# Seven products of half size in the gates of the merge, halved transforms and banded pooling

## The chip, the cores and the metric

The kernel runs on one core of a Trainium2 chip. The metric is the device time of one execution in microseconds; of the kernel before there are three runs, and their median counts. One more execution was profiled; all rows below come from it.

## The reference

Two blocks of two layers each are computed in float32 on 256 context and 256 latent tokens of width 1024. The change touches the second block only, whose mixer takes, in each of its two layers, the normed and modulated tokens `h` and a wide input projection and joins three branches under gates:

```python
k, v, q, u, f, gt = jnp.split(h @ w_in[l], IN_SPLITS, axis=-1)

def multiscale_pool(u, pool_w, pool_scale):     # windows of 2, 4, 8, 16 tokens
    ...
    pooled = (win_sum / cnt - ug).astype(u.dtype)
    y = jnp.einsum('btgc,gcd->btgd', pooled, pool_w).reshape(B, T, POOL_WIDTH)
    return y * pool_scale

def fourier_mix(f):
    ...
    y = jnp.fft.fft2(fg, axes=(1, 3), norm='ortho').real

def merge_branches(o_attn, pool_in, four_in, gate_in, ...):
    g_a, g_p, g_f = jnp.split(jax.nn.sigmoid(gate_in), N_BRANCHES, axis=-1)
    y = (g_a * (o_attn @ w_br_attn)
         + g_p * (multiscale_pool(pool_in, pool_w, pool_scale) @ w_br_pool)
         + g_f * (fourier_mix(four_in) @ w_br_four))
    return y @ w_out
```

The gates are the last 3 x 1024 columns of `h @ w_in`. After the mixer comes a feed-forward part (`w_up`, a convolution over tokens, `w_down`). In layer 0 all 512 tokens pass through mixer and feed-forward, in layer 1 only the 256 latent ones.

## The kernel before

Values lie transposed: features on the 128 partitions, tokens in columns. `hT` holds the normed tokens (8 tiles of 128 features), `brT` the branches (tiles 0 to 3 attention, 4 and 5 pooling, 6 and 7 Fourier), `yT` the merged result. `ps` is PSUM with 8 banks of 512 words. Weights come through a ring of slots of 1 MB in `ring_mem`, loaded by the SP queue; a strip is loaded when the last user of its slot has counted up `strips_used`. Order between engines is written by hand with semaphores. Each engine runs its own program: `merge_tensor` on PE (TensorE), `merge_scalar` on ACT (ScalarE), `merge_vector` on DVE (VectorE), and so on, layer after layer.

In a layer the input projection comes first, then attention in units (lines 1189 to 1337), and with its last unit the other branches:
- `spectra_tensor` (line 1337), issued between the transposes and the values of the last attention unit: for each of two channel tiles and each sequence (two in layer 0, one in layer 1) two matmuls of 512 columns, cosine and sine transform over 256 tokens each.
- `branches_tensor`: pooling as matmuls with a 256 x 256 table (line 1350, `poolm`, two halves of the partitions side by side); `second`, the transform over channels (lines 1360, 1361), for one sequence at a time; the pool weights (line 1366). VectorE copies spectra and pooled values (lines 2363, 2369), ScalarE the results into `brT` (lines 1920, 1925).
- The merge: four turns t of two column tiles m. For each, three gates j of eight matmuls with all tokens (line 1383: 512 columns in layer 0, 256 in layer 1) into banks 0 to 2, and the three branches, 4 + 2 + 2 matmuls (line 1395), into banks 3 to 5. ScalarE makes the sigmoid (line 1936) into `gts`, VectorE multiplies (line 2382) and adds (lines 2385, 2386) into `yT`.
- `out_tensor` (line 1421) with `w_out`, for half of the tokens at a time.

The up stage behind it (`up_tensor`, line 1454) already uses a seven-product form of Strassen's scheme (Winograd's variant). A strip of 1024 x 256 weights is split into four blocks a11, a12 (first 128 columns) and a21, a22, the tokens into two halves. Each of 22 steps does seven products P1 to P7 of four matmuls at half of the tokens, from sums of weight blocks (two by VectorE, lines 2468 and 2469; two by GpSimd, lines 2676 and 2677) and sums of token tiles made once. ScalarE copies P1 (line 1951), and VectorE gathers the results in six sums (lines 2434 to 2442), then does a convolution (line 2451) and the gating. Its products alternate between two sets of four banks, so step f+1 writes one set while f's is gathered.

The values of the last attention unit are line 1311, its copies lines 1906 and 2353. `hT` is completed by ScalarE at line 512.

Of the kernel before, what the change touches and what calls it, by code (L numbers as in the profile page):

```python
# [148 lines left out]
def build(nc, w, const, out):  # L149
# [5 lines left out]
    with ctx:  # L155
# [104 lines left out]
        q_raw = yT[:, 0:4, :]  # L260
        kb = at(T)
        k_rot = at(LAT)
        vb = at(NG * 128).rearrange("p (g c) -> p g c", g=NG)
        ub = at(NG * 256).rearrange("p (g c) -> p g c", g=NG)
        fb = at(NG * 256).rearrange("p (g c) -> p g c", g=NG)
        sc = at(4 * T).rearrange("p (u h t) -> p u h t", u=2, h=2)
# [4 lines left out]
        b_tables = at.at  # L271
        if mla_end > b_tables:
            raise ValueError("the tables lie over the pairs")
# [4 lines left out]
        dftm = at(2 * 512).rearrange("p (s t) -> p s t", s=2)  # L278
# [4 lines left out]
        gts = at(3 * T).rearrange("p (b t) -> p b t", b=3)  # L283
        brg = at(3 * T).rearrange("p (b t) -> p b t", b=3)
# [49 lines left out]
        br_full, br_act_kept, br_dve_kept = sem("br_full"), sem("br_act_kept"), sem("br_dve_kept")  # L334
# [211 lines left out]

        HG_FIRST, HG_ORDER = (2, 3, 0, 4, 1), (2, 4, 0, 3, 1)

        @block.sync
        def _(sp):  # L550
# [80 lines left out]
            for l in range(2):  # L631
# [11 lines left out]
                def merge(j, t):  # L643
                    if j < 3:
                        return [(strip(f"merge{l}", j, 8), wk["w_in_2"][l][:, :, bass.ds(t * 256 + (1280 + j * 1024), 256)])]
# [514 lines left out]
        def base(l):  # L1160
            return dict(unit=16 + 12 * l, ptf=32 + 24 * l, kt=16 + 12 * l, pv=8 + 12 * l, rot=5 + 3 * l, qj=1 + 3 * l, pvk=8 + 4 * l,
                        full=5 * l, act=5 * l, dve=3 + 5 * l, br=12 * l, brd=6 * l, bract=4 * l)
# [168 lines left out]

        def spectra_tensor(pe, l):
            n = 0
            for ct in range(2):
                for s in range(l, 2):
                    for st in range(2):
                        mm = PE.matmul(ps[:, 2 + n, :], fb[:, 2 * s + st, ct * 128:ct * 128 + 128], dftm[:, st, :],
                                       start=st == 0, stop=st == 1)
                    mm.then_inc(br_full, 1)
                    n += 1  # L1340

        def branches_tensor(pe, l):

            b = base(l)
            seqs = range(l, 2)
            for gp in range(2):
                for s in seqs:
                    for st in range(2):
                        for e in range(2):
                            mm = PE.matmul(ps[e * 64:e * 64 + 64, (1, 6)[gp], s * 256:s * 256 + 256],  # L1350
                                           ub[:, 2 * s + st, (2 * gp + e) * 64:(2 * gp + e) * 64 + 64], poolm[:, st, 2 * gp + e, :],
                                           start=st == 0, stop=st == 1)
# [15 lines left out]

        def merge_tensor(pe, l):
            b = base(l)  # L1370
            n, c0 = T - CTX * l, CTX * l
            name = f"merge{l}"
            pe.wait_ge(pv_kept, raised(b["pvk"] + 4))
            with pe.Fori(0, 4) as t:
                for m in range(2):
                    for j in range(3):
                        if m == 0:
                            ring.wait_loaded(pe, name, j, t)
                        if j == 0:
                            pe.wait_ge(gates_ready, raised(t * 6 + (3 * m + 24 * l)))  # L1380
                        wj = strip(name, j, 8)
                        for k in range(8):
                            mm = PE.matmul(ps[:, j, 0:n], wj[:, k, m * 128:m * 128 + 128], hT[:, k, c0:T], start=k == 0, stop=k == 7)  # L1383
                        if m == 0:
                            mm.then_inc(mg_full, 1)
                        else:
                            strip_used(mm)
                    if m == 0:
                        ring.wait_loaded(pe, name, 3, t)
                        pe.wait_ge(br_act_kept, b["bract"] + 4)  # L1390
                    pe.wait_ge(mg_read, raised(t * 2 + (m + 8 * l)))
                    wj = strip(name, 3, 8)
                    for j, (k0, k1) in enumerate(((0, 4), (4, 6), (6, 8))):
                        for k in range(k0, k1):
                            mm = PE.matmul(ps[:, 3 + j, 0:n], wj[:, k, m * 128:m * 128 + 128], brT[:, k, c0:T],  # L1395
                                           start=k == k0, stop=k == k1 - 1)
                        if j < 2 or m == 0:
                            mm.then_inc(mg_full, 1)
                strip_used(mm)

        def wait_merge(eng, l, t, m, bank):
# [1371 lines left out]
```

## Time and profile before

| | us |
|---|---|
| median of three runs | 2563.21 (2562.05 to 2564.33) |
| profiled execution | 2560.08 |
| span of its trace | 2558.3 |
| PE busy | 2489.7 (97%) |
| DVE busy | 1195.6 (47%) |
| ACT busy | 604.2 (24%) |
| POOL busy | 269.0 (11%) |

PE is TensorE's matmuls and PEld its weight loads, which run beside them. A float32 matmul shows as two PE records and two PEld records, and their times overlap those of the next: what a matmul costs in a stream is read from the starts of groups or from the length of a stretch, not from the mean duration of a record. "Idle before" names what ended an idle time. The merges are at 1389.9 to 1609.6 us (layer 0) and 2182.0 to 2292.5 us (layer 1), the up stages at 1666.5 to 1939.9 and 2323 to 2466 us.

### The profile page before, as it was taken

Reading aid. Unit: us, or ns where it says so; the run is one execution under the profiler, and the core shown is the slowest. Engines: PE = TensorE matmul, PEld = TensorE weight load, DVE = VectorE, ACT = ScalarE, POOL = GpSimd, SP = SyncE. Lnnn points to the kernel's source line nnn. Section 1 sums busy time; section 2 is a strip of 40 time slices with the busy share of each in tenths; the row PEclk is TensorE's granted clock in tenths of the full one; section 3 lists DMA queues with packets and bytes.
Section 4 is the critical chain, followed back from the end, with each engine's and each line's share of the span. In section 5 each row is a group of like instructions: output and inputs, shape, how many; then the busy total and the mean of one; then the engine's idle time right before and its main releaser. Section 6 shows DMA issues by size and latency. Waiting matters only on the chain.

```text
span 2558.3 us, 32946 instructions
## 1 busy us (share of the span) xinstructions
PE 2489.7 (97%) x13364; PEld 1947.6 (76%) x13364; DVE 1195.6 (47%) x2007; ACT 604.2 (24%) x1205; POOL 269.0 (11%) x194
## 2 busy tenths in 40 slices
PE   7999999999999898999999999999999999999999
PEld 3688888888887577867885444788885687889998
DVE  3176696696786613343234111256663014116961
ACT  3123233232332113143224000121211023113211
POOL 0011211122121000000000000112120000003410
PEclk9999999999999999999999999999999999999999
DMA  9443343443334042410520222233243132354662
GB/s 357 165 171 139 118 148 116 142 169 115 131 110 137 26 131 82 132 50 23 142 66 1 66 66 90 82 90 85 83 111 85 51 83 66 113 175 124 173 178 63
DMA packets 320673, 284.88 MB, mean 111 GB/s; under 512 B 27137, under 2 KB 300169, under 8 KB 320057
## 3 DMA queue, kind: packets, MB, share of 16 engines
q1 hardware_dynamic: 318810, 279.08, 35.4%
q0 software_dynamic: 1280, 4.20, 0.5%
q8 instruction: 75, 1.23, 0.2%
q14 instruction: 29, 0.24, 0.0%
q10 hardware_dynamic: 479, 0.13, 0.0%
HBM read 280.24 MB, written 3.15 MB: 111 GB/s over the span
## 4 chain that ended last, share of the span: by engine, by line
PE 79%; DVE 13%; issue 3%; ACT 2%; DMA 1%; SPq 0%; DVEq 0%; ACTq 0%
PE ps L1454 11%; PE ps L1383 10%; PE ps L733 7%; PE ps L1533 5%; PE ps L793 4%; PE ps L1521 4%; PE ps L1421 3%; PE ps L1395 3%; PE ps L784 2%; PE ps L917 2%; PE ps L935 2%; PE ps L1012 2%; PE ps L831 2%; DVE arena L2451 2%; DVE arena L2090 2%
## 5 line engine op out<-in xcount | busy, mean ns | idle before, releaser
L1383 PE MATMUL ps<-hT,ring_mem 128*128 128x512 f32 (+1 forms) x768 | 250.3, 486 | 0.0
L1383 PEld LDWEIGHTS ps<-hT,ring_mem 128*128 128x128 f32 x768 | 145.9, 190 | 101.3 <-issue 91.4
L2382 DVE TENSOR_TENSOR arena<-ps,arena 128x512 f32<-128x512 f32 (+1 forms) x48 | 26.8, 558 | 291.3 <-PE ps L1395 291.3
L733 PE MATMUL ps<-xT,ring_mem 128*128 128x256 f32 x672 | 159.8, 381 | 1.6 <-DVE ring_mem L2134 1.4
L733 PE MATMUL ps<-hT,ring_mem 128*128 128x256 f32 x672 | 158.8, 379 | 0.0
L733 PEld LDWEIGHTS ps<-xT,ring_mem 128*128 128x128 f32 x672 | 126.7, 190 | 22.8 <-issue 3.8
L733 PEld LDWEIGHTS ps<-hT,ring_mem 128*128 128x128 f32 x672 | 126.1, 190 | 18.9 <-issue 2.9
L1454 PE MATMUL ps<-hT,arena 128*128 128x256 f32 (+1 forms) x704 | 131.6, 331 | 6.9 <-ACT hT L512 6.9
L831 PE MATMUL ps<-arena,K_c 128*128 128x128 f32 x896 | 120.5, 289 | 11.8 <-ACT K_c L1717 11.7
L831 PEld LDWEIGHTS ps<-arena,K_c 128*128 128x128 f32 x896 | 116.9, 195 | 18.9 <-ACT K_c L1717 11.5
L1454 PE MATMUL ps<-arena 128*128 128x256 f32 (+1 forms) x704 | 129.6, 327 | 0.0
L2391 DVE SCALAR_TENSOR_TENSOR xT<-ps,mod_b,xT 128x256 f32<-128x256 f32 (+1 forms) x60 | 23.6, 427 | 216.0 <-PE ps L1521 88.0
L1454 PEld LDWEIGHTS ps<-hT,arena 128*128 128x128 f32 x704 | 110.7, 193 | 17.5 <-issue 7.5
L1454 PE MATMUL ps<-hT,ring_mem 128*128 128x256 f32 (+1 forms) x704 | 123.0, 327 | 0.0
L443 DVE RECIPROCAL rstd<-root 128x256 f32<-128x256 f32 (+2 forms) x17 | 28.2, 1659 | 199.6 <-ACT root L416 198.5
L2673 POOL TENSOR_TENSOR arena<-ring_mem 128x512 f32<-128x512 f32 x4 | 5.2, 1296 | 1101.5 <-DMA ring_mem<-in_w_up_dram 1101.5
L1521 PE MATMUL ps<-arena,ring_mem 128*128 128x512 f32 (+1 forms) x352 | 115.8, 491 | 2.2 <-DVE arena L2461 2.2
L1454 PEld LDWEIGHTS ps<-arena 128*128 128x128 f32 x704 | 109.7, 191 | 9.1
L1533 PE MATMUL ps<-arena,ring_mem 128*128 128x256 f32 (+1 forms) x704 | 116.6, 327 | 0.0
L1454 PEld LDWEIGHTS ps<-hT,ring_mem 128*128 128x128 f32 x704 | 107.9, 191 | 9.7 <-issue 0.6
L1533 PEld LDWEIGHTS ps<-arena,ring_mem 128*128 128x128 f32 x704 | 106.5, 191 | 10.1 <-issue 1.1
L793 PE MATMUL ps<-ring_mem,hT 128*128 128x256 f32 x512 | 113.0, 379 | 0.0
(316 smaller groups left out, 4302.5 us busy)
## 6 DMA issues: line engine op xcount, KB each, us to landing
ring_mem<-in_w_mod_dram SPq DMA_DIRECT2D x24, 2048.0 KB, 7.7
ring_mem<-in_w_up_dram SPq DMA_DIRECT2D x88, 512.0 KB, 5.2
ring_mem<-in_hg_w_in_dram SPq DMA_DIRECT2D x40, 1024.0 KB, 5.2
ring_mem<-in_w_in_dram SPq DMA_DIRECT2D x30, 1024.0 KB, 5.4
ring_mem<-in_w_down_dram SPq DMA_DIRECT2D x16, 1408.0 KB, 7.0
ring_mem<-in_ada_w_dram SPq DMA_DIRECT2D x8, 2048.0 KB, 7.7
ring_mem<-in_mla_w_in_dram SPq DMA_DIRECT2D x9, 1024.0 KB, 5.5
ring_mem<-in_hg_w_out_dram SPq DMA_DIRECT2D x8, 1024.0 KB, 12.2
```

The lines of the kernel that those rows point to most:

```text
L733: mm = PE.matmul(dst, left[:, k, :], right[:, k, :], start=k == 0, stop=k == 3)
L784: mm = PE.matmul(bank, wj[:, k, m * 128:m * 128 + 128], hT[:, k, :], start=k == 0, stop=k == 7)
L793: mm = PE.matmul(bank[:, g * 256:g * 256 + 256], hT[:, k, tok:tok + 128], wj[:, k, :], start=k == 0, stop=k == 7)
L831: mm = PE.matmul(dst, K_c[:, u * 128:u * 128 + 128], comb(Qw, 1 << (term - 1), u), start=True, stop=True)
L917: mm = PE.matmul(ps[:, 4 - 4 * h + j, 0:256], strip("hg_out", j, 16)[:, k, :], oz[:, k, h * 256:h * 256 + 256], start=k == 0, stop=k == 15)
L935: mm = PE.matmul(ps[:, 4 - 4 * t + j, 0:LAT], strip("mla_out", j, 16)[:, k, :], ozm[:, k, :], start=k == 0, stop=k == 15)
L1383: mm = PE.matmul(ps[:, j, 0:n], wj[:, k, m * 128:m * 128 + 128], hT[:, k, c0:T], start=k == 0, stop=k == 7)
L1395: mm = PE.matmul(ps[:, 3 + j, 0:n], wj[:, k, m * 128:m * 128 + 128], brT[:, k, c0:T], start=k == k0, stop=k == k1 - 1)
L1421: mm = PE.matmul(ps[:, (0 if part == "_a" else 4) + j, m * (hi - lo):(m + 1) * (hi - lo)], wj[:, k, m * 128:m * 128 + 128], yT[:, k, c0 + ...
L1454: mm = PE.matmul(up_region(f, which, hw), left[:, k, :], right[:, k, 0:hw], start=k == 0, stop=k == 3)
L1521: mm = PE.matmul(ps[:, j, 0:n], wj[:, k, :], hid[:, k, 0:n], start=k == 0, stop=k == FT - 1)
L1533: mm = PE.matmul(ps[:, (4 if part == "_a" else 0) + j, 0:hi - lo], wj[:, k, :], hid[:, k, lo:hi], start=k == 0, stop=k == FT - 1)
```

## The change

**Gates.** `merge_tensor` runs 12 steps per layer instead of 4 turns of 2. Step s takes one strip of gate weights (1024 x 256, gate i = s % 3 in the order pooling, Fourier, attention) and does the seven products of the scheme with half of the tokens each, then the two column tiles of the branch that belongs to this gate. In layer 0 the products use banks 0 to 3 in each step, and P1 waits for `mg_gathered` of the step before; in layer 1 they alternate between two pairs of banks and wait for the step before that. VectorE makes two weight sums two steps ahead (`mg_first_vector`), GpSimd the other two. ScalarE copies P1, VectorE gathers into `G_mg`, ScalarE makes the sigmoid in place, VectorE multiplies with the branch in PSUM (`blend`) and sums into `yT`. `out_tensor` waits for the last gather.
**Token sums.** The four sums `T_mg` are made by GpSimd after the last normed token tile (`h_ready`), into a place of their own.
**Transforms.** The table `dftm` keeps 129 cosine and 127 sine columns. The spectra of all sequences of a channel tile share a bank; `second` does one matmul on the cosine parts and one on the sine parts, and ScalarE and VectorE fold them: columns 1 to 127 are even + odd, 255 down to 129 even - odd.
**Pooling.** The matmuls skip columns outside the band: 0 to 136 from the first half of the tokens, 120 to 136 and 136 to 256 from the second.

```diff
         def spectra_tensor(pe, l):
-            n = 0
             for ct in range(2):
                 for s in range(l, 2):
                     for st in range(2):
-                        mm = PE.matmul(ps[:, 2 + n, :], fb[:, 2 * s + st, ct * 128:ct * 128 + 128], dftm[:, st, :],
+                        mm = PE.matmul(ps[:, 2 + ct, s * 256:s * 256 + 256], fb[:, 2 * s + st, ct * 128:ct * 128 + 128], dftm[:, st, :],
...
+        POOLED = ((0, 0, 136, True), (1, 120, 136, False), (1, 136, 256, True))
...
             def second(ct):
-                for i, s in enumerate(seqs):
-                    n = ct * len(seqs) + i
-                    pe.wait_ge(br_dve_kept, b["brd"] + (n + 1 if n < 2 else n + 3))
-                    dst = ps[:, (7, 4)[ct], s * 256:s * 256 + 256]
-                    PE.matmul(dst, dftc[:, 0, :], fcs[:, n % 2, 0:256], start=True, stop=False)
-                    PE.matmul(dst, dftc[:, 1, :], fcs[:, n % 2, 256:512], start=False, stop=True).then_inc(br_full, 1)
+                pe.wait_ge(br_dve_kept, b["brd"] + ct + 1)
+                bank = ps[:, (7, 4)[ct], :]
+                PE.matmul(bank[:, 0:ns * CS], dftc[:, 0, :], view(fcs, (256, ns), (1, CS), at=ct * T + l * 256), start=True, stop=True)
+                PE.matmul(bank[:, ns * CS:ns * 256], dftc[:, 1, :], view(fcs, (256, ns), (1, SN), at=ct * T + l * 256 + CS),
+                          start=True, stop=True).then_inc(br_full, 1)
...
+            for s in range(MS):
+                t, i = divmod(s, 3)
+                ring.wait_loaded(pe, name, i, t)
+                a11, a12, _, a22 = mg_parts(l, s)
+                sums = S_mg[s % 2]
+                if s == 0:
+                    pe.wait_ge(br_dve_kept, 4 * (l + 1))
+                    pe.wait_ge(br_act_kept, 2 * (l + 1))
+                    pe.wait_ge(four_ready, 2 * (l + 1))
+                elif l == 0 or s >= 2:
+                    pe.wait_ge(mg_gathered, MS * l + (s if l == 0 else s - 1))
+                product(s, "P1", a11, hT[:, 0:4, a])
+                product(s, "P2", a12, hT[:, 4:8, a])
+                if s == 0:
+                    pe.wait_ge(mg_turned, 4 * l + 4)
+                product(s, "P4", a22, T_mg[:, 2])
+                pe.wait_ge(mg_first_sums, MS * l + s + 1)
+                product(s, "P7", sums[:, 2], T_mg[:, 0])
+                product(s, "P5", sums[:, 0], T_mg[:, 3])
+                pe.wait_ge(mg_sums, MS * l + s + 1)
+                product(s, "P6", sums[:, 1], T_mg[:, 1])
+                strip_used(product(s, "P3", sums[:, 3], hT[:, 4:8, b_]))
...
+                k0, k1 = ((4, 6), (6, 8), (0, 4))[i]
                 for m in range(2):
...
+                    for k in range(k0, k1):
+                        mm = PE.matmul(ps[:, mg_bank(i) + m, 0:n], wj[:, k, m * 128:m * 128 + 128], brT[:, k, c0:T],
+                                       start=k == k0, stop=k == k1 - 1)
...
             def four(ct):
-                act.wait_ge(br_full, b["br"] + (3 * ns + 2 if ct == 0 else 4 * ns + 4))
-                S.activation(brT[:, 6 + ct, l * 256:T], ps[:, (7, 4)[ct], l * 256:T], ACT.Copy).then_inc(br_act_kept, 1)
+                act.wait_ge(br_full, b["br"] + (5 if ct == 0 else 8))
+                bank = ps[:, (7, 4)[ct], :]
+                S.activation(y_odd[:, ct * 256:ct * 256 + ns * SN], bank[:, ns * CS:ns * 256], ACT.Copy)
+                S.activation(view(brT, (256, ns), (128, 2), at=(6 + ct) * T + l * 256), view(bank, (CS, ns), (128, 2)),
+                             ACT.Copy).then_inc(odd_kept, 1)
...
+            for ct in range(2):
+                dve.wait_ge(odd_kept, 2 * l + ct + 1)
...
+                V.tensor_tensor(view(brT, (256, ns), (1, SN), at=out_ + 1), even, odd, ALU.add)
+                V.tensor_tensor(view(brT, (256, ns), (-1, SN), at=out_ + 255), even, odd, ALU.subtract).then_inc(four_ready, 1)
...
+            def gather(s):
...
+                st.mark(V.tensor_tensor(U(0), P1_mg[:, 0:hw], P("P6"), ALU.add))
+                V.tensor_tensor(C[:, 0, 0:hw], P1_mg[:, 0:hw], P("P2"), ALU.add)
+                st.settle()
+                st.mark(V.tensor_tensor(U(1), U(0), P("P7"), ALU.add))
+                st.mark(V.tensor_tensor(U(2), U(0), P("P5"), ALU.add))
+                st.settle()
+                V.tensor_tensor(C[:, 1, 0:n].rearrange("p (s t) -> p s t", s=2), view(U(1), (0, 2), (1, hw)), mg_pair(l, s, n), ALU.add)
+                V.tensor_tensor(C[:, 0, hw:n], U(2), P("P3"), ALU.add).then_inc(mg_gathered, 1)
...
+            mg_first_vector(dve, l, 1)
+            for s in range(MS):
+                gather(s)
+                if s + 2 < MS:
+                    mg_first_vector(dve, l, s + 2)
+                if s >= 3 and s % 3 == 1:
+                    dve.wait_ge(y_ready, raised(8 * l + 2 * (s // 3)))
+                blend(s)
...
                 attend_vector(dve, st, l)
+                mg_first_vector(dve, l, 0)
                 branches_vector(dve, l)
...
+                a, b, hw = up_halves(l)
+                h_rest, h_top = hT[:, 4:8, b], hT[:, 0:4, b]
+                pool.wait_ge(h_ready, h_end[f"mix{l}_b"])
+                G.tensor_tensor(T_mg[:, 0, :, 0:hw], h_rest, h_top, ALU.subtract).then_inc(mg_turned, 1)
+                G.tensor_tensor(T_mg[:, 3, :, 0:hw], h_top, hT[:, 0:4, a], ALU.subtract).then_inc(mg_turned, 1)
...
+                for s in range(MS):
+                    a11, a12, _, _ = mg_parts(l, s)
+                    sums = S_mg[s % 2]
+                    pool.wait_ge(mg_first_sums, MS * l + s + 1)
+                    steps.link(G.tensor_tensor(sums[:, 1], sums[:, 0], a11, ALU.subtract))
+                    G.tensor_tensor(sums[:, 3], a12, sums[:, 1], ALU.subtract).then_inc(mg_sums, 1)
```

## Rows read from the trace of the kernel before

**Rows 1.** Page, busy shares (us, share of span) and granted clock by slice.
```profile
...
PE 2489.7 (97%) x13364; PEld 1947.6 (76%) x13364; DVE 1195.6 (47%) x2007; ACT 604.2 (24%) x1205; POOL 269.0 (11%) x194
...
PEclk9999999999999999999999999999999999999999
```

**Rows 2.** Busy time by stage; columns: stretch, length, busy (records) by engine, clock, DMA.
```profile
1389.90:1609.60 219.70, 219.70 (x513) 97.27 (x512) 25.59 (x37) 20.06 (x29) 0.00 (x0) 1.00 0.23 72
...
2182.00:2292.50 110.50, 110.50 (x514) 97.27 (x513) 15.73 (x37) 14.71 (x29) 0.00 (x0) 1.00 0.45 139
...
2323.00:2466.00 143.00, 139.91 (x1253) 139.07 (x1252) 124.06 (x298) 33.23 (x93) 51.68 (x40) 1.00 0.63 173
...
1782.73:1794.82 12.09, 12.09 (x57) 10.64 (x56) 7.96 (x14) 2.24 (x4) 2.56 (x2) 1.00 0.33 87
2395.83:2402.08 6.25, 6.25 (x58) 6.25 (x57) 5.79 (x15) 1.37 (x4) 2.57 (x2) 1.00 0.62 170
```

**Rows 3.** What PE waited for, 1180 to 2470 us: total, times, longest.
```profile
...
PE ps L1454 <- ACT hT L512: 6.9, 2, 3.8
```

**Rows 4.** Timeline, layer 0's branches: start, us, engine, line, operands, records.
```profile
...
1373.18 7.03 PE L1337 MATMUL ps<-arena 128*128 128x512 f32 x16
1373.38 0.69 DVE L2353 COPY arena<-ps 128x512 f32<-128x512 f32 x1 [2.58 <-PE ps L1327]
...
1380.14 1.09 PE L1311 MATMUL ps<-arena 128*64 128x128 f32 x16
...
1381.07 3.62 PE L1350 MATMUL ps<-arena 128*64 128x256 f32 x32
...
1384.62 0.70 PE L1360 MATMUL ps<-arena 128*128 128x256 f32 x2
...
1389.89 20.76 PE L1383 MATMUL ps<-hT,ring_mem 128*128 128x512 f32 x48
```

**Rows 5.** Timeline, layer 1's branches, first and last.
```profile
...
2172.98 3.60 PE L1337 MATMUL ps<-arena 128*128 128x512 f32 x8
...
2181.96 10.52 PE L1383 MATMUL ps<-hT,ring_mem 128*128 128x256 f32 x48
```

**Rows 6.** Timeline, one step of layer 0's up stage.
```profile
...
1782.93 0.38 ACT L1951 ACTIVATE root<-ps 128x256 f32<-128x256 f32 x1 [2.08 <-PE ps L1454]
1782.93 0.69 DVE L2468 TENSOR_TENSOR arena<-ring_mem 128x512 f32<-128x512 f32 x1 [4.03 <-PE ps L1454]
1783.54 0.68 DVE L2469 TENSOR_TENSOR arena<-ring_mem 128x512 f32<-128x512 f32 x1
1784.14 0.42 DVE L2434 TENSOR_TENSOR arena<-root,ps 128x256 f32<-128x256 f32 x1
...
1786.19 0.41 DVE L2442 TENSOR_TENSOR arena<-arena,ps 128x256 f32<-128x256 f32 x1
```

**Rows 7.** Timeline and one line's times (min/median/max), layer 1's up stage.
```profile
...
2398.49 0.29 DVE L2434 TENSOR_TENSOR arena<-root,ps 128x128 f32<-128x128 f32 x1 [0.35 <-issue]
...
2399.63 1.29 POOL L2677 TENSOR_TENSOR arena<-ring_mem,arena 128x512 f32<-128x512 f32 x1
2399.74 0.28 DVE L2442 TENSOR_TENSOR arena<-arena,ps 128x128 f32<-128x128 f32 x1
...
L2451 DVE SCALAR_TENSOR_TENSOR arena<-K_c,vecs,arena x36: 471/481/1515, 2348.7 to 2453.1; 128x255 f32<-128x255 f32 x36
```

**Rows 8.** Timeline, tokens normed in layer 0 and VectorE's next work.
```profile
...
1278.34 4.04 ACT L512 ACTIVATE hT<-hT,mod_b,coef 128x256 f32<-128x256 f32 x8 [2.34 <-DVE hT L451]
...
1292.91 0.69 DVE L2291 COPY arena<-ps 128x512 f32<-128x512 f32 x1 [12.31 <-PE ps L1218]
```

**Rows 9.** Loads of strips (KB, us to landing); last operations on y.
```profile
...
ring_mem<-in_w_in_dram SPq DMA_DIRECT2D x30, 1024.0 KB, 5.4
...
1611.40 0.69 DVE L2386 TENSOR_TENSOR arena<-arena 128x512 f32 x1 [0.16 <-DVE arena L2385]
...
2293.70 0.42 DVE L2386 TENSOR_TENSOR arena<-arena 128x256 f32 x1 [0.15 <-DVE arena L2385]
```

More of the change, by code:

```diff
@@ L1344, in branches_tensor @@
             b = base(l)
-            seqs = range(l, 2)
+            ns = 2 - l
             for gp in range(2):
-                for s in seqs:
-                    for st in range(2):
+                for s in range(l, 2):
+                    for st, u0, u1, first in POOLED:
                         for e in range(2):
-                            mm = PE.matmul(ps[e * 64:e * 64 + 64, (1, 6)[gp], s * 256:s * 256 + 256],
-                                           ub[:, 2 * s + st, (2 * gp + e) * 64:(2 * gp + e) * 64 + 64], poolm[:, st, 2 * gp + e, :],
-                                           start=st == 0, stop=st == 1)
+                            mm = PE.matmul(ps[e * 64:e * 64 + 64, (1, 6)[gp], s * 256 + u0:s * 256 + u1],
+                                           ub[:, 2 * s + st, (2 * gp + e) * 64:(2 * gp + e) * 64 + 64], poolm[:, st, 2 * gp + e, u0:u1],
+                                           start=first, stop=u0 > 0)
@@ L1367, in branches_tensor, with mg_bank, mg_parts, mg_region @@
             second(1)
+        MS = 12
+        def mg_bank(i):
+            return 6 if i == 1 else 4
+        def mg_parts(l, s):
+            wj = strip(f"merge{l}", s % 3, 8)
+            return wj[:, 0:4, 0:128], wj[:, 4:8, 0:128], wj[:, 0:4, 128:256], wj[:, 4:8, 128:256]
+        def mg_region(l, s, name, hw):
+            if l == 0:
+                bank, part = {"P1": (0, 0), "P6": (0, 1), "P2": (1, 0), "P7": (1, 1), "P4": (2, 0), "P5": (2, 1), "P3": (3, 0)}[name]
+            else:
+                bank, part = {"P1": (0, 0), "P6": (0, 1), "P2": (0, 2), "P7": (0, 3), "P4": (1, 0), "P5": (1, 1), "P3": (1, 2)}[name]
+                bank = bank + s % 2 * 2
+            return ps[:, bank, part * hw:part * hw + hw]
+        def mg_pair(l, s, n):
+            bank = 2 if l == 0 else s % 2 * 2 + 1
+            return ps[:, bank, 0:n].rearrange("p (s t) -> p s t", s=2)
         def merge_tensor(pe, l):
@@ L1372, in merge_tensor @@
             name = f"merge{l}"
+            a, b_, hw = up_halves(l)
             pe.wait_ge(pv_kept, raised(b["pvk"] + 4))
-            with pe.Fori(0, 4) as t:
-                for m in range(2):
[L1376 to L1399, printed above, removed]
@@ L1401, in wait_merge, with product @@
-        def wait_merge(eng, l, t, m, bank):
-            if m == 1 and bank in (0, 1, 2, 5):
-                wait_strip(eng, f"merge{l}", min(bank, 3), t)
-            else:
-                eng.wait_ge(mg_full, t * 8 + (32 * l + (4 if m else 1) + bank))
+            def product(s, which, left, right):
+                for k in range(4):
+                    mm = PE.matmul(mg_region(l, s, which, hw), left[:, k, :], right[:, k, 0:hw], start=k == 0, stop=k == 3)
+                return mm
+            for s in range(MS):
[20 more added lines that the diff above has]
+                strip_used(product(s, "P3", sums[:, 3], hT[:, 4:8, b_]))
+                if i == 0:
+                    ring.wait_loaded(pe, name, 3, t)
+                if s > (0, 3, 1)[i]:
+                    pe.wait_ge(mg_read, raised(MS * l + s - (0, 2, 1)[i]))
+                wj = strip(name, 3, 8)
+                k0, k1 = ((4, 6), (6, 8), (0, 4))[i]
+                for m in range(2):
+                    for k in range(k0, k1):
+                        mm = PE.matmul(ps[:, mg_bank(i) + m, 0:n], wj[:, k, m * 128:m * 128 + 128], brT[:, k, c0:T],
+                                       start=k == k0, stop=k == k1 - 1)
+                if i < 2:
+                    mm.then_inc(mg_full, 1)
+                else:
+                    strip_used(mm)
@@ new lines, in blend @@
+            def blend(s):
+                t, i = divmod(s, 3)
+                dve.wait_ge(gates_ready, raised(MS * l + s + 1))
+                if i < 2:
+                    dve.wait_ge(mg_full, 8 * l + 2 * t + i + 1)
+                else:
+                    wait_strip(dve, f"merge{l}", 3, t)
+                bank = mg_bank(i)
+                src = ps[:, bank:bank + 2, 0:n]
+                dst = yT[:, 2 * t:2 * t + 2, c0:T]
+                if i == 0:
+                    V.tensor_tensor(dst, src, G_mg[s % 2][:, :, 0:n], ALU.mult).then_inc(mg_read, 1)
+                    return
+                if i == 2:
+                    st.settle()
+                V.tensor_tensor(Y_mg[:, :, 0:n], src, G_mg[s % 2][:, :, 0:n], ALU.mult).then_inc(mg_read, 1)
+                dve.wait_ge(mg_read, raised(MS * l + s + 1))
+                if i == 1:
+                    st.mark(V.tensor_tensor(dst, dst, Y_mg[:, :, 0:n], ALU.add))
+                    return
+                for m in range(2):
+                    V.tensor_tensor(dst[:, m], dst[:, m], Y_mg[:, m, 0:n], ALU.add).then_inc(y_ready, 1)
```

98 lines of the change are left out of this document (59 added, 39 removed).

## The prediction, made before the changed kernel was timed

> **What bounds the kernel now.** I read four views, from coarse to fine. The page's busy shares say which engine could set the time: PE's matmuls cover 97% of the span, the next engine is busy 47%, and the granted clock is 0.9 of full speed or more in all forty slices, so the 2.4 GHz level [rows 1]. The table by stage says whether that holds where the change is: in both merge stages PE is busy for the whole stretch, 219.7 us in layer 0 and 110.5 us in layer 1 [rows 2]. The list of waits says what PE stands for: from the start of the gated layers to the second up stage the longest total is 6.9 us, outside the merge [rows 3]. So the merge is bound by PE, and what leaves PE there leaves the time, unless a new wait takes its place. The timelines then price the pieces. The reader is to see in the rows below that PE's next group starts where the last ends.
>
> **Price of one matmul.** In the merge of layer 0 PE does 256 matmuls of 512 columns (192 for gates, 64 for branches) in 219.7 us: 0.858 us each. In layer 1 it does 256 of 256 columns in 110.5 us: 0.4316 us each [rows 2]. The same seven-product scheme already runs in the up stages, 28 matmuls per step: one step took 12.09 us at 256 columns (0.4318 each) and 6.25 us at 128 columns (0.2232 each), the waits between products included [rows 2].
>
> **Gates by seven products.** Removed per layer: 192 matmuls. Added: 12 steps of 28, each half as wide.
> Layer 0: 12 x 12.09 = 145.1, and the 64 branch matmuls stay at 64 x 0.858 = 54.9; sum 200.0 against 219.7: **-19.7 us**.
> Layer 1: 12 x 6.25 = 75.0, and 64 x 0.4316 = 27.6; sum 102.6 against 110.5: **-7.9 us**.
> The saving in layer 1 is a tenth where it should be an eighth, since 0.2232 is over half of 0.4316. All of it is on PE's path.
>
> **Spectra, pooling, second transform.** The order on PE is last transposes, spectra, values, pooling, second(0), two pool weights, second(1), merge; it ran from 1373.18 to 1389.89 in layer 0, 16.7 us, without a gap over 0.1 us [rows 4], and from 2172.98 to 2181.96 in layer 1, 9.0 us [rows 5]. After, in layer 0: spectra are eight matmuls of 256 columns instead of 512, 3.45. The values keep 0.93 (1380.14 to 1381.07). Pooling is cut from 256 + 256 columns to 136 + 16 + 120 for each pair of halves; nothing in the trace is 16 wide. By columns alone it would be 272/512 of 3.55 (1381.07 to 1384.62), 1.9 us; if a narrow matmul costs as much as a pair of 128 columns in the values (0.93 over four pairs, 0.23) it is 12 x 0.23 = 2.8. I take 2.6, near the upper end, since the values are the same form and the load of the left side doesn't shrink with the columns. The two second transforms cost two matmuls of some 256 columns each instead of four, 0.86 each; the pool weights keep 1.72. Sum 3.45 + 0.93 + 2.6 + 1.72 + 1.72 = 10.4 us, so the last ends at 1383.6, 6.3 earlier.
> **New wait.** Step 0 of the merge now waits on four_ready. Behind second(1) come 0.2 us until ScalarE sees it, its copy of 254 columns (0.38, as the 256-column copy), a small one (under 0.38; 0.2 taken), and two folding sums on VectorE that overlap (0.42 + 0.33, by the gather's 256-column sums [rows 6]), with some 0.1 of hand-over: 1.65 us in which PE stands, all matmuls of the merge queued behind it. Net **-4.6 us**. VectorE's part ahead of it is covered: the first weight sums (1.29 us [rows 6]) run after the copy of the last transposes, from 1374.1 to 1375.4, the first spectra are copied by 1376.1, and PE wants them at about 1380.
> Layer 1: 1.73 + 0.92 + 1.3 + 0.43 + 0.86 + 0.43 = 5.7, and a wait of 1.3 (the tiles are half as wide). That is 7.0 against 9.0: **-2.0 us**. Bounds for both layers together: 1.3 us more gain (pooling by columns), or 3 us less (the folding queued behind something).
>
> **Gather and blend, layer 0.** Its product banks are single, so product P1 of step s+1 waits for the gather of s. Between lie the branch matmuls of s: 4 x 0.858 = 3.43 us in eight steps, twice that in the four steps in which attention's branch runs. The gather, from rows of up0 [rows 6]: 0.2 to ScalarE, copy 0.38, then the chain of six sums from 1784.14 to 1786.60, 2.46, with 0.05: **3.1 us**, cover 3.4, slack 0.3. It is cover by a hair; with none, each of eight steps would pay up to 3.1. I charge 0.5 us for all. VectorE is free at that time: after a gather come weight sums (1.29), the product with the gates (some 1.2 for 1024 columns) and one or two sums, done about 7 us after the products' end, with 15.5 us per step. GpSimd's two sums (1.28 each) are wanted over 8 us after their inputs.
> Layer 1 has two sets of banks, so a gather has a whole step to hide in. VectorE's work there is 1.53 (sums of 128 columns, from 2398.49 to 2400.02 [rows 7]) + 1.29 + two ops of 512 (0.69 each) and hand-overs, about 5 us of 8.0.
>
> **Port shared by VectorE and GpSimd.** In layer 1's up stage a VectorE operation with two SBUF operands took 1.51 us at most against 0.48 in the median, and the slow ones stand behind a GpSimd sum of 1.29 us [rows 7]. So a blend's sum can be held by some 1.0 to 1.3 us when GpSimd's sums start with it; 5 + 1.3 is still under 8.0, and I charge nothing. The gather reads PSUM in all its sums and stayed at 0.28 beside GpSimd. The Trainium skill, SBUF — State Buffer, section SBUF: two separate sides, says that a VectorE operation with two SBUF inputs and a GpSimd one that reads SBUF exclude each other for the whole instruction; by that rule, which the 1.51 us bears out, the sum stays the same but the token sums could hold VectorE for their whole length.
>
> **Token sums on GpSimd.** Four operations of 1024 elements, about 2.6 us each by the 1.28 us of 512: 10 us in layer 0, 5 in layer 1, from the moment when the tokens are normed (1278.34 + 4.04 = 1282.4). VectorE is idle until 1292.91 there [rows 8]; PE wants them 100 us later. GpSimd's later work waits for y in any case. Cost nothing.
>
> **Loads and the end of the merge.** The bytes are the same. In layer 1 a strip is asked for at its slot's last product, takes 5.4 us in the median [rows 9], and is wanted by VectorE some 10 us later; no cost. At the end, y's last tile is ready 2.5 us after PE's last matmul of the merge in layer 0 (1611.40 + 0.69 against 1609.60) and 1.6 in layer 1 now [rows 2, 9]; afterwards about 2.9 and 1.9, while PE's first six or seven matmuls of the output (0.43 or 0.22 each) take 2.6 and 1.3. I charge 0.2 us. ScalarE alternates copy and sigmoid as in the up stages.
>
> **Sum.** -19.7 - 7.9 - 4.6 - 2.0 + 0.5 + 0.2 = -33.5 us. The profiled execution took 2560.08 us (span 2558.3), and would take 2526.6. The median shown is 3.1 higher, 2563.21, and becomes **2529.7 us**.
>
> **Rivals.**
> A. *The hair breaks in layer 0*: the gather starts late (behind the weight sums, as it does in the up stage, +1.29), so 4.4 us against 3.4, eight times: +8 us, 2538. For it: the slack is 0.3. Against: here the gather is first in VectorE's queue. Chance 0.12.
> B. *Layer 1's halves bring nothing*: it needs 192 x 0.4316 / 336 = 0.2466 us per product matmul instead of 0.2232; 2538. The up1 stage as a whole has 139.91 / 616 = 0.227, so 0.05.
> C. *Slower: weight loads no longer hide.* Mechanism: at 128 columns a matmul has two load records of 190 ns to hide (97.27 us for 512) and PE's load side is busy in all of the 6.25 us [rows 2]. If they ran one after another, 0.38 us per matmul, layer 1 would pay 336 x 0.157 = 52.7 us: 2582. It decides from 0.2232 + 33.5/336 = 0.323 us. Against: 28 of the same form took 6.25 us. Chance 0.03. The Trainium skill, TensorE: Matmul & The Clock Gate, section Back-to-back issue gap, gives 81 ns for each pass of 128 columns in a stream of loads and matmuls; taking four passes for float32 (0.858 us for 512 columns at 2.4 GHz is four), an estimate of 0.324 us, layer 1 would lose 34 us and the whole change would come to nothing. The trace has 0.2232 and speaks against it.
> D. *It doesn't do what it says*: PE's waits come in so many places (gather, weight sums, strips) that the eighth is given back, two or three us per step over 12 steps of layer 0; about no change. Chance 0.02.
>
> **Chances and range.** Forecast 0.78 (2526 to 2534), A 0.12, B 0.05, C 0.03, D 0.02. The low end takes the cheap pooling, no gather stall and PE at its best rate; the high end takes A or B with some of the unknown: 2524 to 2539. A measurement of this kernel can tell about 0.2% (5 us) from no change. Faster 0.95, same 0.02, slower 0.03.
>
> **What would show it.** Right: merge stages of about 200 and 103 us; the merge starting 4.6 and 2.0 us sooner after the spectra; PE waits before P1 of step 0 only (1.7, 1.3 us), none before later steps of layer 0; up stages unchanged. Wrong: a wait on VectorE before P1 in eight steps of layer 0 (A); a step of layer 1 over 6.9 us for its seven products (B, C); PE waiting for a strip; the granted clock below its full level inside the merge.

## The result, and the profile after

The changed kernel takes **2532.26 us** in the median of four runs (2528.78 to 2535.14), against 2563.41 for the kernel before in its four: ratio 0.988, 95% interval 0.9865 to 0.9896, 31.2 us less. The forecast was 2529.7. The profiled execution took 2531.50 us (span 2529.6), 28.6 less than that of before, where the sum had said 33.5.

The page after, busy shares, for [rows 1]; PE has lost 36 us of busy time and is as full as before:

```profile
PE 2453.7 (97%) x13956; PEld 2001.4 (79%) x13956; DVE 1271.3 (50%) x2173; ACT 600.8 (24%) x1203; POOL 348.2 (14%) x250
```

What PE waited for after, 1180 to 2470 us (total, times, longest), for [rows 3]:

```profile
PE ps L1501 <- ACT hT L524: 6.9, 2, 3.8
PE ps L1324 <- ACT arena L1953: 3.2, 4, 0.8
PE ps L1414 <- DVE arena L2421: 2.5, 2, 1.4
PE ps L1447 <- DMA ring_mem<-in_w_br_four_dram: 2.4, 2, 1.4
```

The first two lines are the old ones. The third is the foreseen wait of step 0 for the folded transforms (line 2421), 1.4 and 1.0 us. The fourth is new and wasn't foreseen: the branch matmuls (line 1447) wait for their weights. A third such wait of 0.3 us in layer 1 is too short for the list. (The list also has 2.1 us at line 1568, the down projection; that wait is old, 2.15 us at 2475.6 before, where it lay behind the end of the window.)

The timeline after, where the stages begin (spectra, first product, output projection, in each layer), for [rows 4, 5]:

```profile
1373.60 3.62 PE L1352 MATMUL ps<-arena 128*128 128x256 f32 x16
...
1385.52 3.69 PE L1414 MATMUL ps<-hT,ring_mem 128*128 128x256 f32 x16 [1.42 <-DVE arena L2421]
...
1585.57 4.70 PE L1468 MATMUL ps<-arena,ring_mem 128*128 128x256 f32 x21
...
2148.86 1.89 PE L1352 MATMUL ps<-arena 128*128 128x256 f32 x8
...
2155.88 1.35 PE L1414 MATMUL ps<-hT,ring_mem 128*128 128x128 f32 x10 [1.04 <-DVE arena L2421]
...
2261.92 4.29 PE L1468 MATMUL ps<-arena,ring_mem 128*128 128x128 f32 x34
```

Differences of these starts give the stages:

| stage, us | before | forecast | after |
|---|---|---|---|
| layer 0, spectra to merge | 16.7 | 12.1 | 11.9 |
| layer 0, merge | 219.7 | 200.0 | 200.05 |
| layer 1, spectra to merge | 9.0 | 7.0 | 7.0 |
| layer 1, merge | 110.5 | 102.6 | 106.0 |

Three of four are within 0.2 us. The merge of layer 1 lost 3.4 us of its 7.9: the starts of its branch matmuls in steps 3, 6 and 9 are 1.6, 0.3 and 1.1 us late, and the matmuls behind each such wait take some 0.1 us longer. Another 1.6 us went where nothing was changed: the up stage of layer 1, from its first product to the first matmul of the down projection, took 143.9 us instead of 142.3. In both traces PE waits 3.1 us for the normed tokens there; after, the granted clock then falls, before it doesn't. The windows of 8 us from 2 to 3 us ahead of the end of that wait, first before, then after; the first value after the busy times is the clock:

```profile
2328.00:2336.00 8.00, 5.88 (x49) 5.71 (x50) 3.95 (x11) 3.13 (x8) 0.00 (x0) 1.00 0.01 2
```
```profile
2297.00:2305.00 8.00, 5.34 (x30) 5.17 (x31) 4.44 (x13) 3.19 (x8) 0.00 (x0) 0.79 0.01 3
```

A mean of 0.79 over 8 us is some 3.4 us at the lower level (1.2 GHz), 1.7 us lost. So two questions were open: why the weights come late, and whether the clock's fall belongs to the change.

### The profile page after: what moved, and what is told of

The parts are those of the page before. It is cut to its first block, busy times and chain, and to the rows that moved or that the text cites. A ratio compares the mean times of both kernels' runs of the same rounds, so it can differ in the third digit from the quotient of the medians.

```text
span 2529.6 us, 34129 instructions
## 1 busy us (share of the span) xinstructions
PE 2453.7 (97%) x13956; PEld 2001.4 (79%) x13956; DVE 1271.3 (50%) x2173; ACT 600.8 (24%) x1203; POOL 348.2 (14%) x250
## 4 chain that ended last, share of the span: by engine, by line
PE 78%; DVE 13%; issue 4%; ACT 2%; DMA 1%; SPq 1%; DVEq 0%; ACTq 0%
PE ps L1501 11%; PE ps L1414 8%; PE ps L746 7%; PE ps L1580 5%; PE ps L806 4%; PE ps L1568 4%; PE ps L1468 3%; PE ps L1447 3%; PE ps L797 2%; PE ps L930 2%; PE ps L948 2%; PE ps L1025 2%; PE ps L844 2%; DVE arena L2549 2%; DVE arena L2141 2%
## 5 line engine op out<-in xcount | busy, mean ns | idle before, releaser
L746 PEld LDWEIGHTS ps<-hT,ring_mem 128*128 128x128 f32 x672 | 126.1, 190 | 18.9 <-issue 2.9
L844 PE MATMUL ps<-arena,K_c 128*128 128x128 f32 x896 | 120.6, 289 | 11.9 <-ACT K_c L1764 11.8
L1501 PE MATMUL ps<-arena 128*128 128x256 f32 (+1 forms) x704 | 130.1, 328 | 0.0
L1501 PEld LDWEIGHTS ps<-hT,ring_mem 128*128 128x128 f32 x704 | 107.9, 191 | 9.7 <-issue 0.6
L1580 PEld LDWEIGHTS ps<-arena,ring_mem 128*128 128x128 f32 x704 | 106.5, 191 | 10.1 <-issue 1.1
L1568 PEld LDWEIGHTS ps<-arena,ring_mem 128*128 128x128 f32 x352 | 67.8, 193 | 49.5 <-issue 41.4
L806 PEld LDWEIGHTS ps<-ring_mem,hT 128*128 128x128 f32 x512 | 96.1, 190 | 12.4
L2790 POOL TENSOR_TENSOR arena<-arena,ring_mem 128x512 f32<-128x512 f32 x44 | 56.1, 1276 | 333.3 <-DVE arena L2567 333.3
L1414 PE MATMUL ps<-arena 128*128 128x256 f32 (+1 forms) x576 | 98.2, 327 | 0.0
```

The source lines that it names most:

```text
L746: mm = PE.matmul(dst, left[:, k, :], right[:, k, :], start=k == 0, stop=k == 3)
L806: mm = PE.matmul(bank[:, g * 256:g * 256 + 256], hT[:, k, tok:tok + 128], wj[:, k, :], start=k == 0, stop=k == 7)
L844: mm = PE.matmul(dst, K_c[:, u * 128:u * 128 + 128], comb(Qw, 1 << (term - 1), u), start=True, stop=True)
L1414: mm = PE.matmul(mg_region(l, s, which, hw), left[:, k, :], right[:, k, 0:hw], start=k == 0, stop=k == 3)
L1501: mm = PE.matmul(up_region(f, which, hw), left[:, k, :], right[:, k, 0:hw], start=k == 0, stop=k == 3)
L1568: mm = PE.matmul(ps[:, j, 0:n], wj[:, k, :], hid[:, k, 0:n], start=k == 0, stop=k == FT - 1)
```

## The experiments

Each ran together with the kernel before on one chip. Differences among the changed kernels are of 1 to 3 us, while the times of one kernel spread over 2 to 9 us and not all kernels ran on the same chip. So the readings below rest on the lengths of stages, taken from the starts in each kernel's timeline as above, and the medians only accompany them. A stand is a time in which PE has work and waits.

**The changed kernel once more**, as a base.

> The changed kernel once more, as the base of the others. Theory: of the 4.8 us by which its profiled execution missed the forecast, 2.6 us are PE waiting for the branches' weights in layer 1's merge and will be there again (three waits, 1.4, 0.3 and 0.9 us, before the branch matmuls of steps 3, 6 and 9); some 1.7 us were a fall of PE's granted clock to its lower level at the start of the up stage of layer 1, which comes and goes between executions. Rival: the 1.7 us belong to the change (its different instruction order before the up stage), and then the low stretch at the start of that stage is there again. Median 2529 to 2534.

Median 2531.96 us. The stages are 11.92, 200.05, 7.02 and 106.46 us; the waits for the branches' weights come to 2.9 us, and the fall of the clock is there again (143.9 us). The rival on the clock stands so far. The profiled execution took 2535.55 us, 4.0 more than the one above; 2.7 of them lie ahead of the first spectra, where nothing was changed.

**Step 0 waits later.**

```diff
-                    pe.wait_ge(br_act_kept, 2 * (l + 1))
-                    pe.wait_ge(four_ready, 2 * (l + 1))
...
                 product(s, "P6", sums[:, 1], T_mg[:, 1])
+                if s == 0:
+                    pe.wait_ge(br_act_kept, 2 * (l + 1))
+                    pe.wait_ge(four_ready, 2 * (l + 1))
```

> One edit: in step 0 of each merge PE no longer waits for the pooled and folded branches before product P1 but before P3. Theory (the wait before P1 is all that stands there): the stands of 1.4 us in layer 0 and 1.0 us in layer 1 are gone, the merges start that much sooner after the second transform, nothing else moves: -2.4 us, about 2530. Rival (the gather of step 0 or the weight sums of step 1, which stand behind the folding on VectorE, now come late): PE waits as long at P7 or P1 of step 1, same time as the changed kernel.

Median 2530.29 us, 1.7 below the base; by stages 10.34 and 5.81 us from the spectra to the merge (-1.6, -1.2) and 199.97 and 106.08 for the merges. Its timeline shows VectorE's folding beside the first products:

```profile
1386.40 3.62 PE L1414 MATMUL ps<-hT,ring_mem 128*128 128x256 f32 x16
...
1387.08 0.42 DVE L2421 TENSOR_TENSOR arena<-ps,arena 128x254 f32<-128x254 f32 x1 [1.83 <-ACT arena L1970]
1387.42 0.41 DVE L2422 TENSOR_TENSOR arena<-ps,arena 128x254 f32<-128x254 f32 x1
```

The stand was all that the wait cost, and nothing behind it came late. The stages give 2.8 us and the median 1.7, within its spread.

**The branches' weights in three parts.** First the place of the wait in the changed kernel, SP's queue and PE in layer 1:

```profile
2182.01 1.43 SPq L133 DMA_DIRECT2D ring_mem<-in_w_br_attn_dram  x2
2183.62 0.46 SPq L133 DMA_DIRECT2D ring_mem<-in_w_br_pool_dram  x1
2184.18 0.42 SPq L133 DMA_DIRECT2D ring_mem<-in_w_br_four_dram  x1
```
```profile
2178.16 3.62 PE L1447 MATMUL ps<-arena,ring_mem 128*128 128x256 f32 x16
...
2181.62 1.95 PE L1414 MATMUL ps<-hT,ring_mem 128*128 128x128 f32 x16
...
2186.98 1.06 PE L1414 MATMUL ps<-hT,arena 128*128 128x128 f32 x8
...
2189.47 1.99 PE L1447 MATMUL ps<-arena,ring_mem 128*128 128x256 f32 x8 [1.44 <-DMA ring_mem<-in_w_br_four_dram]
```

The slot is free when the attention branch of a turn is done, at 2181.62. Four loads are issued, the last at 2184.18, and land by about 2189.4: 7.8 us. PE wants them after the seven products of the next step, 6.25 us later. In layer 0 these products last 12.1 us and cover the load. In the kernel before, 24 gate matmuls came first, 24 x 0.4316 = 10.4 us [rows 2]. The edit asks for each part when its own last user is done:

```diff
-                ring.fill(sp, f"merge{l}", merge)
+                for t in range(4):
+                    for j in range(3):
+                        sp.wait_ge(strips_used, st_["first"] + 4 * (t - 1) + j + 1 if t else st_["need"][j])
+                        for dst, src in merge(j, t):
+                            sp.dma_start(dst, src).then_inc(loaded[j], 16)
...
+                        elif t and j < 2:
+                            sp.wait_ge(mg_full, 8 * l + 2 * (t - 1) + j + 1)
+                        elif t:
+                            sp.wait_ge(strips_used, st_["first"] + 4 * t)
+                        for dst, src in merge(3, t)[j:j + 1] if j < 2 else merge(3, t)[2:]:
+                            sp.dma_start(dst, src).then_inc(br_loaded[j], 16)
...
-                if i == 0:
-                    ring.wait_loaded(pe, name, 3, t)
+                pe.wait_ge(br_loaded[i], (16, 16, 32)[i] * (4 * l + t + 1))
```

> One edit: the branches' weights of a turn are no longer asked for in one go when the last of them has been used, but in three parts, each when its own last user of the turn before is done (pooling, Fourier, attention), with a semaphore for each. Theory (layer 1's products last 6.3 us, and the load takes longer than that): the three waits of layer 1 are gone, its merge takes 103.0 to 103.5 us instead of 106.0; layer 0 stays at 200.0. Rival (the queue of loads as a whole is too slow in layer 1, the bytes and not the moment of asking): the waits move to the gate strips or stay, 105 us or more.

Median 2529.42 us, 2.5 below the base; layer 0's merge 200.05, layer 1's 102.74 us, against a forecast of 102.6. The same bytes in the same queue, and PE is busy in all of it:

```profile
2158.86:2261.60 102.74, 102.74 (x800) 99.44 (x801) 48.60 (x115) 12.17 (x25) 29.21 (x22) 1.00 0.49 150
```

So the bytes and the bandwidth weren't the limit, and the whole gap of the stage is closed. Which part of the edit did it isn't shown: besides asking earlier it puts pooling's and Fourier's parts ahead of attention's two, and PE waits for its own part only, where it waited for all four loads although step 3 needs pooling's alone. No run changed only one of these.

**Both edits.**

> Both edits. If they are independent: -2.4 and -2.6, 5.0 us below the changed kernel, about 2527.5, and clear of both kernels.

Median **2526.02 us** (2523.55 to 2527.69), ratio to the kernel before 0.9861 (0.9845 to 0.9878), 5.9 below the base. The stages are 10.33, 199.98, 5.81 and 102.67 us, each as with the one edit that bears on it: the two are independent.

**Weight sums ahead of the gather**, rival A's mechanism made on purpose.

```diff
-                gather(s)
                 if s + 2 < MS:
                     mg_first_vector(dve, l, s + 2)
+                gather(s)
```

> One edit: VectorE makes the two weight sums of step s+2 before it gathers step s, as the up stage does, not after. Theory (layer 0's gather hides under 3.43 us of branch matmuls with 0.3 us to spare): in the eight steps whose branch has four matmuls PE stands for about 1.0 us before P1, in the other four not, so layer 0's merge takes 208 us instead of 200; layer 1, with two sets of banks, stays as it is (106). Rival (the cover isn't that tight, or PE's wait costs nothing because the semaphore is checked ahead of time): 200 to 202 us.

Median 2537.45 us. Layer 0's merge takes 205.13 us: 5.1 more, not 8. One of the eight steps in this kernel (step 0), and then one in the changed kernel (step 1, whose branch has as many matmuls):

```profile
1401.02 3.60 PE L1447 MATMUL ps<-arena,ring_mem 128*128 128x512 f32 x8
...
1401.29 0.69 DVE L2428 TENSOR_TENSOR arena<-ring_mem 128x512 f32<-128x512 f32 x1 [11.38 <-PE ps L1414]
...
1402.50 0.41 DVE L2445 TENSOR_TENSOR arena<-root,ps 128x256 f32<-128x256 f32 x1
...
1404.55 0.41 DVE L2452 TENSOR_TENSOR arena<-arena,ps 128x256 f32<-128x256 f32 x1
...
1405.11 3.69 PE L1414 MATMUL ps<-hT,ring_mem 128*128 128x256 f32 x16 [0.49 <-DVE arena L2452]
```
```profile
1413.20 3.60 PE L1447 MATMUL ps<-arena,ring_mem 128*128 128x512 f32 x8
...
1413.87 0.42 DVE L2445 TENSOR_TENSOR arena<-root,ps 128x256 f32<-128x256 f32 x1 [10.69 <-ACT root L1985]
...
1415.92 0.41 DVE L2452 TENSOR_TENSOR arena<-arena,ps 128x256 f32<-128x256 f32 x1
...
1416.63 3.62 PE L1414 MATMUL ps<-hT,ring_mem 128*128 128x256 f32 x16
```

In the changed kernel the gather ends 3.13 us after the branch's matmuls start (1416.33 against 1413.20) and PE goes on at 3.43: the slack of 0.3 us is real. The sums ahead move the gather's start only from 0.67 to 1.48 us, since they run beside ScalarE's copy of P1; the step pays 0.66 us (4.09 from the branch's start to P1 instead of 3.43). The mechanism was as stated, its price too high: the expectation added the sums to a copy that they overlap. Layer 1's merge took 108.8 us where 106 was expected, with 3.6 us of waits for weights and a fall of the clock behind the longest of them (2.3 us).

**Layer 1's gates by full matmuls again.**

```diff
-                merge_tensor(pe, l)
+                (merge_tensor if l == 0 else plain_tensor)(pe, l)
```

(`plain_tensor`, `plain_scalar` and `plain_vector` are the merge of the kernel before.)

> One part undone: layer 1's gates are made by 192 full matmuls of 256 columns again, in the old order; layer 0 and all branches stay as changed. Theory: layer 1's merge takes 110.5 us again, against 106.0 with seven products and late weights and 103 with early ones; the wait before its first product is gone too (the branches are wanted later there), 1.0 us. So 3.5 us over the changed kernel. Rival (halves of 128 columns bring nothing in layer 1, as 0.2466 us per product would mean): the same time as the changed kernel or less.

Median 2534.18 us. Layer 1: 5.82 us to the merge, which has no wait ahead of it, and 110.51 us in it; together 116.3, against 113.1 in the changed kernel and 108.5 with both edits. Rival B falls: halves of 128 columns do pay, 7.8 us once the weights come in time. The expectation was 3.5 us over the changed kernel; the stages give 3.3, the medians 2.2.

**The branches' part alone**, on the kernel before.

```diff
-                        pe.wait_ge(br_act_kept, b["bract"] + 4)
+                        pe.wait_ge(br_act_kept, b["bract"] + 2)
+                        pe.wait_ge(four_ready, 2 * l + 2)
```

(and all hunks of the change that touch spectra, pooling and the second transform.)

> The kernel before with the halved transforms and the banded pooling alone; all gates by full matmuls. The branches are awaited before the first branch matmuls, 24 gate matmuls after the start of the merge. Theory (PE's matmuls are all that counts there): the stretch from the spectra to the merge takes 10.5 us instead of 16.7 in layer 0 and 6.0 instead of 9.0 in layer 1, with no stand: -9.2 us, about 2552. Rival (VectorE and ScalarE chain sets the end): less than half of that.

Median 2552.93 us, 8.7 below the kernel before. The stretches take 10.34 and 5.81 us, -9.5 us together (-9.2 was expected), and the merges 219.73 and 110.51, as before; 1.6 us of the gain go to the clock's fall in the up stage of layer 1, which is here too, though this merge has no product of half size.

**Token sums on VectorE**, after the branches instead of on GpSimd long before.

```diff
-                G.tensor_tensor(T_mg[:, 0, :, 0:hw], h_rest, h_top, ALU.subtract).then_inc(mg_turned, 1)
...
+            turned_vector(dve, l)
             mg_first_vector(dve, l, 1)
```

> One edit: the four token sums of the merge are made by VectorE after the branches instead of by GpSimd as soon as the tokens are normed. Theory (GpSimd's sums cost nothing because they are made 100 us ahead): VectorE needs about 1.25 us for each of four sums of 1024 elements in layer 0 and 0.7 in layer 1, less P1 and P2 (3.5 and 1.8 us) which run meanwhile; the weight sums of step 1 aren't wanted by then, so PE stands 1.5 to 2.5 us before P4 of step 0 in layer 0 and 1.0 to 1.5 in layer 1: +3 us. Rival (GpSimd's early sums slow something in the input stage, and that gain outweighs): the same time or less.

Median 2533.6 us, 1.6 above the base. PE stands before P4 of step 0, 1.0 us in layer 0 and 0.5 in layer 1:

```profile
1385.24 1.21 DVE L2435 TENSOR_TENSOR arena<-hT 128x1024 f32<-128x1024 f32 x1
...
1388.88 1.23 DVE L2440 TENSOR_TENSOR arena<-hT,arena 128x1024 f32<-128x1024 f32 x1
...
1390.16 1.99 PE L1414 MATMUL ps<-arena,ring_mem 128*128 128x256 f32 x8 [1.00 <-DVE arena L2440]
```

Layer 0's merge took 201.32 us against 200.05: 1.3 us, where 1.5 to 2.5 was expected, and in layer 1 the stand was 0.5 where 1.0 to 1.5 was expected. The mechanism was as stated, its price too high. With GpSimd nothing waited for these sums: they were free.

**Whose is the fall of the clock?** The kernel before twice more, and then with the matmuls of layer 1's spectra done two or four times over (the same result, 3.4 and 10.3 us more work for PE ahead of the stage):

> The kernel before, unchanged, profiled a second time. In the first profile its granted clock stays at 1.00 through the start of layer 1's up stage, while every profile of a changed kernel so far has a stretch of some 4 us near 0.6 there, worth 1.7 us, after the same wait of 3.1 us. Theory (the low stretch comes and goes in all kernels): it is there in one or both of the two new profiles, and the stage from the output's end to the last stage is 1.5 to 2 us longer than in the first. Rival (it comes with the change): 1.00 in both.

> The kernel before, unchanged, profiled a third time; as the second.

> The kernel before, with the matmuls of layer 1's spectra done twice (the same result, four matmuls more, 3.4 us): its up stage in layer 1 starts 3.4 us later, with nothing else changed. The question is the stretch of low clock behind that stage's first wait (3.1 us), seen in all nine profiles of changed kernels and in none of three of the kernel before. Theory (it hangs on the moment at which this wait falls, not on what the merge does): in this or the next run the clock falls there, and the stage is 1.7 us longer. Rival (it hangs on the changed work ahead of it): 1.00 in both.

```diff
-                    for st in range(2):
+                    for st in tuple(range(2)) * (1 + (l == 1) * 1):
```

> The same with the spectra of layer 1 done four times, 10.3 us later. As the run before it.

2560.80, 2561.40, 2566.39 and 2571.13 us, one execution each. The up stage of layer 1 took 142.3 us in both profiles of the kernel before, 143.9 with 3.4 us more ahead of it, and 142.3 again with 10.3 us more. The windows of 8 us, first for 3.4 us, then for 10.3 us:

```profile
2332.00:2340.00 8.00, 5.46 (x30) 5.29 (x31) 4.36 (x12) 3.18 (x8) 0.00 (x0) 0.79 0.02 5
```
```profile
2338.00:2346.00 8.00, 4.91 (x41) 4.60 (x40) 5.02 (x13) 3.18 (x8) 0.00 (x0) 1.00 0.12 37
```

So both simple theories fall. It doesn't come and go at random (three profiles of the kernel before without it, nine of changed ones with it), and it doesn't need the changed work: the old kernel with 3.4 us more ahead has it. The wait is 3.1 us long in all of them. That its moment decides isn't shown either: in the nine changed profiles it ended at moments from 2293.9 to 2322.2 us, and all nine have the fall. So the cause stays open. It cost 1.6 us in eight of the nine and 2.4 in the run with token sums on VectorE (144.7 us), where the low stretch was twice as long.

Other falls are in the kernel before too. Its clock is low behind the wait of 3.8 us in layer 0's up stage and behind that of 2.15 us before the down projection of layer 1, and the same two places have it in all fourteen profiles. Two windows of the kernel before:

```profile
1678.00:1686.00 8.00, 6.96 (x24) 5.61 (x25) 5.40 (x6) 2.37 (x5) 0.00 (x0) 0.79 0.00 0
2474.00:2482.00 8.00, 6.43 (x22) 5.33 (x23) 2.72 (x7) 0.73 (x2) 0.00 (x0) 0.79 0.44 124
```

So what was new in the changed kernels is a third place, not the fall itself.

## Why the prediction was right, and where it was off

**The bound.** "What leaves PE there leaves the time, unless a new wait takes its place" held. Of the 4.9 us between the forecast and the trace (33.5 and 28.6) 3.4 are the unforeseen wait and 1.6 the clock; the small rest is told under the balance. The median missed by only 2.6 us, and that is luck: the forecast put the median 3.1 us above the profiled execution, as before, and after the change it is 0.8 above.

**The price of a matmul.** 0.4318 and 0.2232 us were taken from the up stages for another stage of the same form. Layer 0's merge came out at 200.05 us for a sum of 200.0, and layer 1's at 102.7 for 102.6 once its weights were in time. The waits between products cost what they cost in the up stage.

**Spectra, pooling, second transform.** Sum and new wait came to 11.9 and 7.0 us, for 12.1 and 7.0. The stand of 1.65 us was 1.4, and 1.3 was 1.0. Pooling took 2.32 us (1378.07 to 1380.39 in the timeline after) where 2.6 was taken between 1.9 and 2.8: the matmuls of 16 columns are cheaper than those of 128, but far from free. The two second transforms came out at 0.97 and 1.03 us where 0.86 each was taken, so small misses cancelled in the sum.

```profile
1378.07 2.38 PE L1364 MATMUL ps<-arena 128*64 128x136 f32 x48
...
1380.39 0.70 PE L1372 MATMUL ps<-arena 128*128 128x258 f32 x2
```

**Gather and blend.** Forecast 3.1 us under a cover of 3.43 with 0.3 to spare; measured 3.13. The 0.5 us charged for it wasn't needed, nor the 0.2 at the end of the merge. The run with sums first shows that this hair matters, at 0.66 us for each of eight steps.

**Loads: the step that failed.** It said "In layer 1 a strip is asked for at its slot's last product, takes 5.4 us in the median [rows 9], and is wanted by VectorE some 10 us later; no cost". That holds for the three gate strips. The fourth, the branches' weights, has its last user at the end of a turn and its first one step later, 6.25 us, while it takes 7.8 us to come back, 2.2 of them for SP to issue four loads. The run with three parts shows it in full: 3.3 to 3.7 us. The change moved the first use of that slot from behind 24 gate matmuls to behind one step, and the prediction looked at its bytes only. The diff had it: the branch of gate 0 now comes in step 0 of a turn.

**Port shared by VectorE and GpSimd.** Expected to hold some of the blend's sums, at no cost. In layer 1 the sum of 512 elements (line 2472) took 1.26 us in the median where the fastest of the four took 0.69:

```profile
L2472 DVE TENSOR_TENSOR arena<-arena x4: 692/1258/1268, 2174.1 to 2254.1; 128x512 f32<-128x512 f32 x4
```

Neither merge lost time to it: layer 0's ended at its sum, and layer 1's did once its weights came in time. The Trainium skill, SBUF — State Buffer, section SBUF: two separate sides, has the loser blocked for the whole instruction; the trace agrees in kind. In layer 0 it was GpSimd that was held, 2.13 us instead of 1.28:

```profile
1418.72 1.26 DVE L2472 TENSOR_TENSOR arena<-arena 128x1024 f32<-128x1024 f32 x1
1418.97 2.13 POOL L2776 TENSOR_TENSOR arena<-ring_mem,arena 128x512 f32<-128x512 f32 x1
```

**Rivals.** A wasn't the case (no wait on the gather in any step of the changed kernel) but its mechanism exists, at 5.1 us instead of 8. B and C fall by 102.7 us for layer 1's merge. Of D's waits one came true, that for the weights, in three steps of layer 1.

**The balance.** The four stages gave 30.9 us in the trace, the clock took 1.6 back, and 0.7 lie in stretches that weren't changed (0.4 of them before the first spectra). That leaves the 28.6 measured. The 0.7 us that the sum charged for gather and output weren't used by them, and happen to match this rest.

## What to carry to other kernels

Price a moved algorithm by a stage of the same kernel that already runs it at the same width, waits and all; here that was good to 0.1 us in 200. When steps are regrouped, list for each buffer its last user and its next first user, with the time between them and the time that a refill takes from the moment of asking, issue of every load included: the total of bytes says nothing about it. A wait placed before the first of seven products can be moved down to the first one that needs it. And ask of every wait whether it asks for more than the next matmuls read. Where the times of one kernel spread more than the effect, compare the lengths of stages.

## What the runs showed of the hardware

- The granted clock can fall to its lower level behind a wait of 3.1 us that has the same length and the same work around it in another kernel where it stays at 1.00; 3.4 us later it fell and 10.3 us later not (one profile each). It cost 1.6 us, once 2.4. Comparisons of a few microseconds carry such a step.
- A wait for weights of 2.3 us in the middle of layer 1's merge (the run with sums first) was followed by low clock as well (a mean of 0.79 over 8 us), waits of 0.3 to 1.7 us for weights in the other kernels were not. Before the down projection of layer 1 waits of 2.05 to 2.4 us were followed by it in all fourteen profiles, those of the kernel before included. A short stand can so cost more than its length.
- Matmuls of 16 columns with a left side of 64: pooling in layer 0 takes 2.32 us in twelve pairs of which eight are 120 or 136 wide. With these eight at 0.23, as the values' [rows 4], the four narrow pairs cost about 0.12 each, an estimate, where their share of columns (16 of 128 in 0.23) would give 0.03.
